# Residual x transposed by DMA ahead of its use, and the output projection's weight sums on GpSimd

## What is computed

```python
h = rmsnorm(x, norm_mix)
(a_b, a_c, a_x, qb, kb, vb, qc, kc, vc, qi, ki, wi, g_a, g_b, g_c) = split(h @ w_in)
br_a = (a_b * causal_dwconv(a_c * a_x, conv_a)) @ w_a_out      # gated short convolution
br_b = sliding_window_attention(qb, kb, vb, sinks) @ w_swa_o   # 8 heads, 2 kv heads
br_c = top_k_sparse_attention(qc, kc, vc, qi, ki, wi) @ w_dsa_o
merged = sigmoid(g_a) * br_a + sigmoid(g_b) * br_b + sigmoid(g_c) * br_c
x = x + merged @ w_out                                         # the residual sum of this case
h2 = rmsnorm(x, norm_ffn)
x = x + (silu(causal_dwconv(h2 @ w_gate)) * (h2 @ w_up)) @ w_down
y = rmsnorm(x, norm_final)
```

## Time and profile before

| | |
|---|---|
| median of 3 runs | 1750.12 us |
| span of the profiled execution | 1748.6 us |
| granted TensorE clock | 0.996 (mean of the span) |
| TensorE matmuls busy | 1717.8 us, 98% |
| VectorE busy | 1341.5 us, 77% |
| ACT busy | 757.8 us, 43% |
| GpSimd (POOL) busy | 579.4 us, 33% |

### The profile page before, as it was taken

One profiled execution on the slowest core, in us unless ns is written; L12 is line 12 of the kernel. 1 busy time (PEld: TensorE's weight loads), 2 busy tenths in 40 slices (PEclk: granted clock), 3 DMA queues, 4 the chain that ended last, 5 costly groups with the idle time before them and its releaser, 6 DMA issues.

```text
span 1748.6 us, 32318 instructions
## 1 busy us (share of the span) xinstructions
PE 1717.8 (98%) x12275; PEld 1678.6 (96%) x12275; DVE 1341.5 (77%) x2193; ACT 757.8 (43%) x1333; POOL 579.4 (33%) x466
## 2 busy tenths in 40 slices
PE   6999999999999999999999999999999999999998
PEld 6999999999999999888899999999999999999998
DVE  6689899978799996778759989666666665865765
ACT  5344333368621234767734563333333333422334
POOL 2211842266745431000021102655455554121130
PEclk9999999999999999999999999999999999999999
DMA  4101111111243415422324112222222223533112
GB/s 157 49 25 43 49 43 48 49 38 28 68 137 124 128 40 171 144 85 85 109 71 151 49 49 61 87 85 75 74 80 80 87 74 111 167 117 112 61 37 100
DMA packets 179190, 146.43 MB, mean 84 GB/s; under 512 B 10140, under 2 KB 149676, under 8 KB 179052
## 3 DMA queue, kind: packets, MB, share of 16 engines
q1 hardware_dynamic: 178076, 142.54, 26.3%
q0 software_dynamic: 976, 2.00, 0.5%
HBM read 118.22 MB, written 26.28 MB: 83 GB/s over the span
## 4 chain that ended last, share of the span: by engine, by line
PE 91%; DVE 4%; ACT 2%; issue 1%; DMA 1%; POOL 1%; SPq 0%; DVEq 0%; ACTq 0%; POOLq 0%
PE ps L1602 28%; PE ps L2079 23%; PE ps L2152 7%; PE ps L2138 7%; PE ps L1714 5%; PE ps L1775 4%; PE ps L1795 4%; PE ps L1614 4%; PE ps L2009 3%; PE ps L1921 3%; PE ps L1869 1%; PE ps L1632 1%; PE ps L1876 1%; ACT probs L2537 0%; DMA x_rows<-in_x_prompt 0%
## 5 line engine op out<-in xcount | busy, mean ns | idle before, releaser
L3171 DVE MAX8 top<-key_mask 128x8 f32<-128x1024 f32 (+5 forms) x166 | 151.8, 917 | 9.7 <-DVE key_mask L3171 3.4
L1602 PE MATMUL ps<-h_hi,w_hi 128*128 128x352 f32 (+1 forms) x720 | 158.0, 327 | 0.0
L1602 PE MATMUL ps<-h_hi,w_lo 128*128 128x352 f32 (+1 forms) x720 | 155.2, 323 | 0.0
L1602 PE MATMUL ps<-h_lo,w_hi 128*128 128x352 f32 (+1 forms) x720 | 154.8, 323 | 0.0
L1289 POOL TENSOR_TENSOR w_lo<-w_raw,w_hi 128x512 fp32r<-128x512 f32 (+1 forms) x43 | 79.3, 1843 | 217.4 <-ACT w_hi L2240 217.3
L3171 DVE MATCH_REPLACE8 key_mask<-top,key_mask 128x1024 f32<-128x1024 f32 (+5 forms) x166 | 149.4, 904 | 0.3 <-issue 0.3
L2079 PE MATMUL ps<-mix_hi,quarter_hi 128*128 128x264 f32 x672 | 136.9, 285 | 0.2 <-ACT x_one L2240 0.2
L2079 PE MATMUL ps<-mix_hi,quarter_lo 128*128 128x264 f32 x672 | 136.4, 284 | 0.0
L2079 PE MATMUL ps<-mix_lo,quarter_hi 128*128 128x264 f32 x672 | 136.0, 284 | 0.0
L1602 PEld LDWEIGHTS ps<-h_hi,w_hi 128*128 128x128 f32 (+1 forms) x720 | 120.6, 187 | 2.6 <-issue 0.9
L1602 PEld LDWEIGHTS ps<-h_hi,w_lo 128*128 128x128 f32 (+1 forms) x720 | 122.5, 186 | 0.5
(11 more groups left out here) (452 smaller groups left out, 5017.5 us busy)
## 6 DMA issues: line engine op xcount, KB each, us to landing
w_raw<-in_w_in SPq DMA_DIRECT2D x54, 256.0 KB, 3.0
w_hi<-gate_highs SPq DMA_DIRECT2D x48, 256.0 KB, 2.8
w_lo<-gate_lows SPq DMA_DIRECT2D x48, 256.0 KB, 3.0
ffn_tiles<-t SPq DMA_DIRECT2D x44, 264.0 KB, 2.4
w_raw<-in_w_gate SPq DMA_DIRECT2D x44, 256.0 KB, 3.1
w_raw<-in_w_up SPq DMA_DIRECT2D x44, 256.0 KB, 3.1
w_raw_in_lo<-in_w_in SPq DMA_DIRECT2D x30, 256.0 KB, 3.0
w_raw<-in_w_down SPq DMA_DIRECT2D x32, 192.0 KB, 2.8
```

What stands on the lines that cost most here:

```text
L1602: last = nc.tensor.matmul(PS[0:rows, NB * k + b, 0:e - a], w[:, k, t, 0:rows], x[:, t, a:e], start=m == 0 and w is WHI and x is hi, stop=m ...
L3171: step.mark(V_.max(top, s) if find else V_.match_replace(s, top, s, TAKEN))
```

## The change

- TensorE's 72 transposes of x and ACT's nine copies of them go, with the load of XR. In their place, in the stage of the window branch's gates, SP issues for each feature tile j two DMA transposes of x's float32 read as 2-byte halves (`x_turn`), stores the turned halves to HBM (`x_bounce`) and loads them back with the two halves of each number on one partition (`x_plane_load`); ACT interleaves them to float32 (`x_column`), and SP stores the column tile to HBM (`x_store`, X_TILES). In the output projection SP loads the 8 tiles straight into X2 (`residual_load`).
- The low part of job J_WO + 1, the clearing of T0 and all twelve weight sums of `out_weights` move from VectorE to GpSimd. GpSimd's order is then: low part of J_WO + 1; clear T0; sums of m = 1; `mix_early` 0 and 1; sums of m = 2; `mix_early` 2 and 3; sums of m = 3.

```diff
+            def x_turn(j):
+                at = bass.ds(j * (2 * P), 2 * P)
+                sp.dma_start_transpose(X_TURNED[:, :, 0:SEQ], x_halves(ins["x_prompt"])[:, at]).then_inc(xt_turned, 16)
+                sp.dma_start_transpose(X_TURNED[:, :, SEQ:TOK], x_halves(ins["x_sample"])[:, at]).then_inc(xt_turned, 16)
+            def x_bounce(j):
+                sp.wait_ge(xt_turned, 32 * j + 32)
...
+                sp.dma_start(X_HALVES[at, :].rearrange("(c p) t -> p c t", p=P), X_TURNED[:, :, :]).then_inc(xt_halves, 16)
+            def x_plane_load(j):
+                sp.wait_ge(xt_halves, 16 * j + 16)
...
+                sp.dma_start(X_PLANES[:, :, :], X_HALVES[at, :].rearrange("(p h) t -> p h t", h=2)).then_inc(xt_planes, 16)
+            def x_store(j):
+                sp.wait_ge(xt_columns, landed(j + 1))
...
+                sp.dma_start(X_TILES[bass.ds(j, 1), :, :].rearrange("a p t -> p (a t)"), X_COLUMNS[:, :]).then_inc(xt_stored, 16)
...
-                with sp.Fori(1, KT) as j:
...
+                first_loads(1)
+                sp.wait_ge(pv_done, WINDOW[-1]["q"] + len(WINDOW[-1]["chunks"]))
+                x_turn(0)
+                second_loads(1)
+                third_load(1)
+                x_bounce(0)
+                x_plane_load(0)
+                x_turn(1)
+                with sp.Fori(2, KT) as j:
+                    first_loads(j)
+                    x_bounce(j - 1)
+                    x_store(j - 2)
+                    second_loads(j)
+                    x_plane_load(j - 1)
+                    third_load(j)
+                    x_turn(j)
+                x_bounce(KT - 1)
...
+                    if n0 == J_C and k == 0:
+                        x_store(KT - 2)
+                        x_plane_load(KT - 1)
                 if n0 == J_C:
                     gate_store(KT - 1)
+                    x_store(KT - 1)
...
-            sp.wait_ge(job_done, J_WO - 1)
-            for i in range(0, NT, 2):
...
+            def residual_load(j):
+                sp.wait_ge(sum_ready, max(SPARSE_ORDER.index(j), SPARSE_ORDER.index(j // 2)) + 1)
+                sp.dma_start(X2[:, j, :], X_TILES[j]).then_inc(xr_in[j // 2], 16)
+            sp.wait_ge(xt_stored, landed(16 * KT))
+            for j in (0, 1, 3, 2):
+                residual_load(j)
...
-            for n in range(J_BC + 2, J_WO + 1):
+            for n in range(J_BC + 2, J_WO + 2):
                 split(0, n // 2, n % 2, tiles=tiles_of(n))
+            pool.wait_ge(m_lo, KT)
+            pool.wait_ge(d_raw[2], KH)
+            nc.gpsimd.memset(T0[:, 0:TOK], 0.0).then_inc(ssq_sum, 1)
+            def out_weights(m):
+                for half in range(2):
+                    pool.wait_ge(out_in[half], 32 * m)
...
+                nc.gpsimd.tensor_tensor(out_source(m, Q_S1), A21, A22, ALU.add).then_inc(pair_sum, 1)
...
+            out_weights(1)
+            mix_early(0)
+            mix_early(1)
+            out_weights(2)
+            mix_early(2)
+            mix_early(3)
+            out_weights(3)
...
-            project(J_WO, 0, 0, M_HI, M_LO, ready=(m_lo, 0), order=SPARSE_ORDER,
-                    between={t: x_tile(t - 3) for t in range(3, KT)})
-            project(J_WO, 0, 1, M_HI, M_LO, between={t: x_tile(t + 5) for t in range(4)})
+            project(J_WO, 0, 0, M_HI, M_LO, ready=(m_lo, 0), order=SPARSE_ORDER)
+            project(J_WO, 0, 1, M_HI, M_LO)
...
+            def x_column(j):
+                act.wait_ge(xt_planes, landed(16 * j + 16))
+                act.wait_ge(xt_stored, landed(16 * j))
...
+                copy(X_COLUMNS[:, :].bitcast(U16).rearrange("p (t h) -> p t h", h=2),
+                     X_PLANES[:, :, :].rearrange("p h t -> p h t")).then_inc(xt_columns, 1)
...
-            V_.memset(T0[:, 0:TOK], 0.0).then_inc(ssq_sum, 1)
...
-            dve.wait_ge(lo_ready, J_WO)
-            following(J_WO, 0, 0)
...
             mix_t_raw(3)
-            out_weights(1, *SUMS)
-            dve.wait_ge(xr_out, 5)
             mix_t_raw(4)
-            dve.wait_ge(xr_out, NT + 1)
```

More of the change, by code:

```diff
@@ L28 @@
 BF16 = mybir.dt.bfloat16
+U16 = mybir.dt.uint16
 P = 128
@@ L297, in build @@
         Y = place("y", [P, NT + 1, D], F32, 24)
-        XR = place("x_rows_again", [P, NT + 1, D], F32, 24)
+        X_TURNED = place("x_halves_turned", [P, 2, TOK], U16, 38)
+        X_PLANES = place("x_half_planes", [P, 2, TOK], U16, 39)
+        X_COLUMNS = place("x_columns", [P, TOK], F32, 40)
         A_HI = place("a_hi", [P, CT, TOK], F32R, 24)
@@ L596, in tile_rows, with x_halves @@
             return a.rearrange("r (t p) -> (r t) p", p=P)
+        def x_halves(x):
+            return x[0].bitcast(U16)
         def x_rows(i):
@@ L1142, in _ @@
                         sp.dma_start(dst, src).then_inc(out_in[half], 16)
+                if m == 1:
+                    for j in range(4, KT):
+                        residual_load(j)
             sp.wait_ge(pair_lo, out_count(OUT_PAIRS[-1], Q_A22))
@@ L1485, in _ @@
             sparse_split(len(SPARSE), 0)
-            for n in range(J_BC + 2, J_WO + 1):
+            for n in range(J_BC + 2, J_WO + 2):
                 split(0, n // 2, n % 2, tiles=tiles_of(n))
+            pool.wait_ge(m_lo, KT)
[4 more added lines that the diff above has]
+                    pool.wait_ge(out_in[half], 32 * m)
+                if m > 1:
+                    pool.wait_ge(pair_lo, out_count(m - 1, Q_S1))
+                nc.gpsimd.tensor_tensor(out_source(m, Q_S1), A21, A22, ALU.add).then_inc(pair_sum, 1)
+                if m > 1:
+                    pool.wait_ge(pair_lo, out_count(m - 1, Q_S2))
+                pool.wait_ge(pair_sum, out_sums(m, Q_S1))
+                nc.gpsimd.tensor_tensor(out_source(m, Q_S2), OUT_SUM[Q_S1][:, :], A11, ALU.subtract).then_inc(pair_sum, 1)
+                if m > 1:
+                    pool.wait_ge(pair_lo, out_count(m - 1, Q_S4))
+                pool.wait_ge(pair_sum, out_sums(m, Q_S2))
+                nc.gpsimd.tensor_tensor(out_source(m, Q_S4), A12, OUT_SUM[Q_S2][:, :], ALU.subtract).then_inc(pair_sum, 1)
+                if m > 1:
+                    pool.wait_ge(pair_done, out_count(m - 1, Q_S3))
+                nc.gpsimd.tensor_tensor(out_source(m, Q_S3), A11, A21, ALU.subtract).then_inc(pair_sum, 1)
             def mix_early(j):
@@ L1546, in pair_sums @@
                 nc.gpsimd.tensor_tensor(DSUM[Q_S3][:, :], a21, a11, ALU.subtract).then_inc(pair_sum, 1)
-            for j in range(KH):
-                mix_early(j)
+            out_weights(1)
[5 more added lines that the diff above has]
+            out_weights(3)
             pool.wait_ge(ss_var, 1)
@@ L2457, in sparse_gates, with gate @@
                     split(0, n // 2 + 1, n % 2, tiles=CT)
+            def x_column(j):
+                act.wait_ge(xt_planes, landed(16 * j + 16))
+                act.wait_ge(xt_stored, landed(16 * j))
+                apart(act)
+                copy(X_COLUMNS[:, :].bitcast(U16).rearrange("p (t h) -> p t h", h=2),
+                     X_PLANES[:, :, :].rearrange("p h t -> p t h")).then_inc(xt_columns, 1)
             def gates(n0):
-                with act.Fori(0, KT) as j:
+                def gate(j):
                     following(n0, j, 0, tiles=CT)
@@ L2467, in gates @@
                     following(n0, j, 1)
+                gate(0)
+                with act.Fori(1, KT) as j:
+                    gate(j)
+                    x_column(j - 1)
+                x_column(KT - 1)
             def attention_jobs(n0, side, r_c, k_tiles):
@@ L2472, in attention_jobs @@
                 done(n0, 0, 0)
+                if n0 == J_C:
+                    act.wait_ge(xt_stored, landed(16 * KT))
                 if n0 == J_B:
@@ L2710, in _ @@
             mix_t_high(1, *T_ORDER[:3])
[L2711 to L2715, removed]
             out_high(1, Q_A11, Q_S1)
@@ L3637, in mix_t_raw @@
                                      op).then_inc(d_raw[d], 1)
[L3639 to L3653, removed]
             def out_low(m, *which):
```

36 lines of the change are left out of this document (16 added, 20 removed).

## The result

The changed kernel takes 1753.93 us (median of 9 runs, 1752.5 to 1757.7), the kernel before 1750.27 beside it (9 runs, 1749.53 to 1752.99): ratio 1.0021, 95% interval 1.0012 to 1.0029. Forecast were 1752.5 us and 1742 to 1757.5. It is slower by 3.7 us, at the edge of the 0.2% that I had called distinguishable. The span of the profiled execution is 1751.0 us (1752.8 with what lies around it), as forecast; but it is made up otherwise than I had said.

What follows compares the result with a forecast made beforehand. TensorE, 98% busy, bounds the kernel, with VectorE equally full in the output projection up to 994. Span 1748.6 + 2.4 (2.5 - 0.1; gates' stage 0) = 1751.0, plus 1.5 to the median: 1752.5 us, range 1742 to 1757.5.

Steps and rivals of the forecast that it cites:

- TensorE, 7.77 us to gain: Output projection: the 72 transposes hold 7.77 us of TensorE's path, the most that can be gained.
- VectorE to the third product, +2.5 us of work, product 1.3 later: Output projection: 5.70 us leave VectorE, 2.3 + 4.7 + 1.2 come; third Strassen product starts 1.3 us later.
- the 1.2 us for `mix_early(0)`: Output projection: `mix_early(0)`, now free after `residual(0)`, meets the low parts and costs VectorE 1.2 us (0 to 1.27).
- the slack of 1.34 us: Before the change, from VectorE's end of S2's low part (972.17) to TensorE's third product (973.51): 1.34 us.
- the signs that I had named: First product about 965.4, waits before it and the third, mixes stretched in turn with GpSimd's sums, no gates' stage wait.
- First product at 965.4: Output projection: TensorE's first Strassen product begins about 965.4, after 963.5, the residual sum and one low part.
- Second pair, -0.1: Output projection: -2.65 of sums, +3.1 of lock-outs, -0.55 of idle give -0.1, leaving VectorE and TensorE 2.4 us late.
- Third pair absorbed: Output projection: the third pair's exchange, +2.1 us, fits in VectorE's 5.4 us idle, and TensorE runs through.
- Gates' stage, 0: Stage of the gates: transposes, DMAs and ACT copies put between the others cost 0.
- I take 5 us: hidden by 9.8: Gates' stage, SP's queue: a transpose pair takes 5 us, hidden by 9.8 us free before ACT reads the load.
- 13.4 of 17.5 us: End of gates' stage: ACT's chain with x_column(7) takes 13.4 us while TensorE has 17.5 us of tiles to run.
- Late residual tiles: Output projection rival: residual tiles land late from HBM and `residual(0)` waits, 3 us; chance 0.03.

Runs made afterwards that it cites:

- clears: The changed kernel with the four weight sums of m = 1 not computed, GpSimd clearing their tiles instead: 1750.30 us, ratio 1.0001 to the kernel before.
- turned_part: The changed kernel with the low part of J_WO + 1, the clearing and all twelve sums back on VectorE: 1751.98 us, ratio 1.0007.
- vector_fed: vector_sums with unread matmuls filling TensorE's two waits, 18 ahead of the first Strassen product and 16 ahead of the third: 1747.56 us, ratio 0.9981.
- store_late: load_first with each round's column-tile store and next half-plane loads issued behind the two weight loads, not ahead of them: 1751.84 us, ratio 1.0004.
- load_first: The changed kernel with job J_C's first weight load issued ahead of the last pair of transposes and its store: 1752.28 us, ratio 1.0010.
- gpsimd_fed: store_late with unread matmuls in TensorE's waits, 38 ahead of the first Strassen product and 18 ahead of the third: 1751.30 us, ratio 1.0003.
- vector_sums: store_late with all twelve weight sums and the low part of J_WO + 1 on VectorE, only the clearing on GpSimd: 1748.71 us, ratio 0.9986.

## Why the prediction was right, and where it was not

- **TensorE, 7.77 us to gain.** clears, turned_part and vector_fed bear it out as a bound: the less VectorE has to do, the earlier TensorE goes on, and the best of them came 3.2 us under the kernel before. In the changed kernel itself TensorE was ready for the first product at 967.16 - 5.21 = 961.95, which is 960.03 on the old clock (less 1.92 us, by which the output stage began later), 7.6 us before the 967.64 of before.
- **VectorE to the third product, +2.5 us of work, product 1.3 later.** Lock-out by the low part: 2.2 (said 2.3). By four sums: 4.4 (said 4.7). Clearing: 0, shown by clears. The step that failed is the 1.2 us for `mix_early(0)`: it cost nothing more than before. GpSimd's first subtraction waited through VectorE's whole row of mixes, and the second took its 1.2 us from the same two mixes as before the change (2.45 for 2.55). With 2.2 + 4.4 - 5.70 = +0.9 the low part of S2 ends at 974.84 - 1.92 = 972.92 on the old clock, 0.75 late, and the product starts 0.2 late. I had also left out that this product waits for VectorE's next instruction, the add of A11 (974.76 + 0.69 = 975.45; product 975.61): of the slack of 1.34 us only 0.7 was real. And of the signs that I had named one did not show: there was no wait ahead of the third product, and TensorE stood for 5.2 us and not for 9. In place of the rest it ran 5.6 us of work at half the clock.
- **First product at 965.4.** 967.16 - 1.92 = 965.24.
- **Second pair, -0.1.** Between the third products it was +0.9, on VectorE's way +0.4: VectorE was 0.75 late at the low part of S2 and 1.11 late here (997.46 - 1.92 - 994.43). The lock-outs sum to 3.8 us (2.31 for 1.25; two low parts at 1.78 for 0.68; three in 2.38 for 1.88) where I had counted 3.1; -2.65 + 3.8 - 0.55 = +0.6. The other 0.5 or so of the 0.9 is the slack at the first pair's third product, which had hidden that much of VectorE's 0.75, and here none is left.
- **Third pair absorbed.** Right: TensorE is busy 35.00 of 35.00.
- **Gates' stage, 0.** Wrong, and the largest miss: +2.3. The step that failed is "I take 5 us: hidden by 9.8". I had priced a pair of transposes as something that lands, and let the 9.8 us before the load's reader cover it. But it first holds the queue: 3.2 to 6.3 + 1.2 us of issuing (4.5 to 4.9 in the changed kernel from the third on), where two ordinary loads take 0.96. Two things follow that I did not look for: the round's loop through SP's queue and ACT became longer than the round (store_late), and at the end of the stage I followed `x_column(7)` on ACT, 13.4 of 17.5 us, and not the plain weight load behind it in the queue (load_first).
- **Late residual tiles.** Right to give it little: no instruction of VectorE waits for a transfer between 930 and 1035.
- **Not foreseen: the clock.** It fell to half within the 5.2 us wait. In the changed kernel most of that lay where TensorE would have waited for VectorE, so the sum did not need it (gpsimd_fed).

That 1752.5 came so near is thus in part luck, two misses that cancel: 2.3 us too little in one stage; in the other 1.3 too much, 2.4 for 1.1. The mechanism of the output stage is shown: VectorE is the bound there, and work handed to GpSimd came back as a lock-out of at least its own length (0.66 us of a sum against 1.1; 1.2 us of a low part against 2.2). The prices of the Trainium skill for the transposes were both off: "VectorE: DVE Perf Modes", The three transpose paths, would have made a pair 21.6 us (estimated from its 1309 ns a block); it landed in 6.6 + 2.3. "Advanced Engine Details and Errata", X-Bar Transpose (TRN2), calls them as fast as ordinary transfers; the plain transfers of as many bytes beside them landed in 2.7 to 4.5 us.

Open: why GpSimd and VectorE alternate in the sums (951.53) and not at the first subtraction of `mix_early(0)` (966.56). No run tells it apart.

## What to carry to other kernels

When an instruction is added to a queue, price its issuing and its landing separately, and follow every later entry of that queue, above all the plain loads of the next stage; then close the loop through the engines that the queue waits for, and compare its length with the round. Before work is handed from VectorE to GpSimd, see whether it reads SBUF beside a VectorE instruction with two SBUF inputs: the sums and the low part, which do, gave VectorE nothing back here, and only the clearings, which just write, were free. When one engine is relieved and then waits for another, look at the granted clock within the wait and behind it.

## What the runs showed of the hardware that was not expected

- A DMA transpose of 1024 x 256 two-byte numbers held the issuing queue for 3.2 to 6.3 us over the runs (3.2 to 3.6 for the first two, 3.9 and more for the rest), a plain transfer of 528 KB for 0.33 to 0.74; the transpose landed 6.6 us after its issue (median of eight; 6.6 to 7.2 by run).
- TensorE's clock fell to half within a single wait of 5.2 us, 4.0 us into it in the changed kernel and 2.7 in store_late, and stayed there for the first 5.6 and 4.3 us of work. After waits of 2.42 and 2.25 us, 6 us apart, it fell 1.3 us after work had been taken up again, for 3.4 us (vector_sums). With the same waits filled with unread matmuls, down to 0.3 us each, it did not fall (vector_fed).
- A clearing on GpSimd did not delay VectorE at all; a sum that takes GpSimd 1.3 us by itself delayed it by 1.1.
